# Depthwise convolution of a transformer kernel: all eight channel tiles' filter sums on TensorE, between the tiles of the product ahead of it

## The reference, cut to what matters

```python
def conformer_conv(h, w_pw1, b_pw1, w_dw, b_dw, ln_g, ln_b, w_pw2, b_pw2):
    u = h @ w_pw1 + b_pw1                    # (256, 1024) @ (1024, 2048)
    a, gate = jnp.split(u, 2, axis=-1)
    u = a * jax.nn.sigmoid(gate)             # 1024 channels
    u = causal_depthwise_conv(u, w_dw) + b_dw    # width 31, each channel by itself
    u = jax.nn.silu(layernorm(u, ln_g, ln_b))    # mean and variance over the channels
    return u @ w_pw2 + b_pw2
```

## Time and profile before

| | us or share |
|---|---|
| the profiled execution's own time | 1320.58 |
| its span in the trace | 1319.2 |
| TensorE busy | 1213.2 (92%) |
| VectorE busy | 959.4 (73%) |
| ScalarE busy | 653.0 (49%) |
| mean granted TensorE clock | 0.972 |
| last matmul of pw1 starts at | 69.45 |
| TensorE's convolution begins, mean's last matmul done | 69.66, about 103.6 |
| last matmul of pw2 starts at | 137.21 |

### The profile page before, as it was taken

One profiled execution on the slowest core, in us unless ns is written; L12 is line 12 of the kernel. 1 busy time (PEld: TensorE's weight loads), 2 busy tenths in 40 slices (PEclk: granted clock), 3 DMA queues, 4 the chain that ended last, 5 costly groups with the idle time before them and its releaser, 6 DMA issues.

```text
span 1319.2 us, 24769 instructions
## 1 busy us (share of the span) xinstructions
PE 1213.2 (92%) x9796; PEld 1152.0 (87%) x9796; DVE 959.4 (73%) x1853; ACT 653.0 (49%) x1142; POOL 109.0 (8%) x106
## 2 busy tenths in 40 slices
PE   5988899999998999999977878999988778999999
PEld 4957899999987999999866778999988667999999
DVE  5966598869776888779896558888875554766743
ACT  5316554445446544445556545445445664544531
POOL 2000100002000200004001112000011122100000
PEclk9989899999999999999998989999989988999999
DMA  7587687877853687777633326777855322555551
GB/s 275 158 192 104 209 306 255 260 261 267 265 168 130 217 263 254 248 264 259 212 107 103 96 80 205 260 265 243 301 183 176 117 88 81 181 187 179 189 191 65
DMA packets 81127, 259.36 MB, mean 197 GB/s; under 512 B 8905, under 2 KB 20425, under 8 KB 81013
## 3 DMA queue, kind: packets, MB, share of 16 engines
q1 hardware_dynamic: 81012, 257.79, 61.5%
HBM read 252.68 MB, written 5.08 MB: 195 GB/s over the span
## 4 chain that ended last, share of the span: by engine, by line
PE 70%; DVE 18%; ACT 5%; issue 3%; DMA 1%; POOL 0%; DVEq 0%; ACTq 0%
PE ps L521 63%; DVE wlo L1188 6%; DVE CV L1194 1%; PE ps L582 1%; DVE X L1194 1%; DVE aacc L1194 1%; ACT HH L840 1%; DMA raw<-wall 1%; PE ps L617 1%; ACT tmp L840 1%; ACT oS L840 1%; DVE tmp L1532 1%; PE ps L621 1%; DVE HL L1188 1%; PE ps L689 1%
## 5 line engine op out<-in xcount | busy, mean ns | idle before, releaser
L521 PE MATMUL ps<-HH,whi 128*128 128x256 f32 (+1 forms) x2152 | 626.6, 291 | 32.5 <-DVE wlo L1188 12.5
L521 PE MATMUL ps<-HH,wlo 128*128 128x256 f32 (+1 forms) x2152 | 616.1, 286 | 0.0
L521 PE MATMUL ps<-HL,whi 128*128 128x256 f32 (+1 forms) x2152 | 615.8, 286 | 0.0
L840 ACT ACTIVATE whi<-raw 128x1024 fp32r<-128x1024 f32 x363 | 381.0, 1057 | 335.9 <-PE ps L521 332.1
L1188 DVE TENSOR_TENSOR wlo<-raw,whi 128x1024 fp32r<-128x1024 f32 x363 | 444.2, 1229 | 38.0 <-ACT whi L840 37.6
L521 PEld LDWEIGHTS ps<-HH,whi 128*128 128x128 f32 x2152 | 417.0, 194 | 51.3 <-issue 19.6
L521 PEld LDWEIGHTS ps<-HL,whi 128*128 128x128 f32 x2152 | 416.9, 194 | 0.6
L521 PEld LDWEIGHTS ps<-HH,wlo 128*128 128x128 f32 x2152 | 416.3, 193 | 0.0
L521 PE MATMUL ps<-GH,whi 128*128 128x256 f32 x704 | 198.5, 282 | 0.6 <-DVE bcol L1414 0.5
L521 PE MATMUL ps<-GL,whi 128*128 128x256 f32 x704 | 197.8, 281 | 0.0
L521 PE MATMUL ps<-GH,wlo 128*128 128x256 f32 x704 | 197.8, 281 | 0.0
(11 more groups left out here) (207 smaller groups left out, 976.7 us busy)
## 6 DMA issues: line engine op xcount, KB each, us to landing
raw<-wall SPq DMA_DIRECT2D x363, 512.0 KB, 4.2
araw<-ada SPq DMA_DIRECT2D x96, 512.0 KB, 4.7
UR<-uscr SPq DMA_DIRECT2D x24, 142.0 KB, 3.2
scratch<-bvec SPq DMA_DIRECT2D x1, 3072.0 KB
oBB<-kbias SPq DMA_DIRECT2D x16, 192.0 KB, 2.5
aTB<-scratch SPq DMA_DIRECT2D x12, 128.0 KB, 2.5
X<-x_in SPq DMA_DIRECT2D x2, 512.0 KB, 5.8
out<-X SPq DMA_DIRECT2D x8, 128.0 KB, 2.9
```

What stands on the lines that cost most here:

```text
L521: ins = pe.e.matmul(o, l, r, start=(kt == p.order[0] and i == 0), stop=(kt == p.order[-1] and i == 2))
L840: ac.then_inc(ac.e.activation(o, i, func, **kw), sem)
```

## The change

- All eight channel tiles are convolved by TensorE. VectorE's 62 tap instructions are gone.
- Channel tile j is convolved behind pw1 tile 2j + 5 (`TAPS_AFTER = 4`), so tiles 0 to 5 lie between the tiles of pw1 or right behind its last, 6 and 7 behind that. Directly behind channel tile j stands one matmul of the channel sum, for tile j - 1. Only the sum of tile 7 stands at the end.
- DG becomes a ring of three (it waits for the convolution three before), and VectorE writes U ahead of DG. ScalarE's CV copies move in between its pw1 steps.
- SyncE: U is written out at nt = 2j + 2 and read back at nt = 2j + 3, for all eight; no reads are left for behind the loop. The 3 MB write still stands behind the last of them.

```diff
-CONV_DVE = (0, 1)
-CONV_PE = tuple(j for j in range(KD) if j not in CONV_DVE)
+TAPS_AFTER = 4
@@ TensorE
+                def taps(j):
+                    bk = bank[5 + j % 2]
+                    pe.wait_ge(S.dg, j + 1)
+                    pe.wait_ge(S.ur[j % 3], 64 * (j // 3 + 1))
+                    if j >= 2:
+                        pe.wait_ge(S.cva, j - 1)
+                    for m in range(8):
+                        for r in range(4):
+                            ins = pe.e.matmul(bk[32 * r:32 * r + 32, 0:T], DG[j % 3][:, 8 * r + m, :],
+                                              UR[j % 3][:, r, 4 * m:4 * m + T], start=(m == 0), stop=(m == 7))
+                    pe.then_inc(ins, S.cvt)
+                    if j:
+                        channel_sum(j - 1)
+                def channel_sum(j):
+                    pe.wait_ge(S.bv, 1)
+                    pe.wait_ge(S.cva, j + 1)
+                    return pe.e.matmul(bank[7][:, 0:T], ones[:, :], CV[:, j, :], start=(j == 0), stop=(j == KD - 1))
                 def after(nt):
+                    j, odd_tile = divmod(nt - TAPS_AFTER, 2)
+                    if odd_tile and j >= 0:
+                        taps(j)
...
-                for n, j in enumerate(CONV_PE):
...
+                for j in range((16 - TAPS_AFTER) // 2, KD):
+                    taps(j)
+                pe.then_inc(channel_sum(KD - 1), S.lnt)
@@ VectorE
-                    if nt >= 4:
-                        for _ in range(4):
-                            tap()
...
                         stt(U[:, n, 30:30 + T], t[:, :], V("bp1", n), TMP[(nt - 1) % 8][:, :], ALU.add, ALU.mult, S.u)
+                        dv.wait_ge(S.wq, 16)
+                        dv.wait_ge(S.id32, 3)
+                        if n >= 3:
+                            dv.wait_ge(S.cvt, n - 2)
+                        tt(DG[n % 3][:, :, :], id32[:, :].unsqueeze(1).broadcast_to([P, 32, 32]),
+                           wq[:, n, :].unsqueeze(2).broadcast_to([P, 32, 32]), ALU.mult, S.dg)
-                while taps:
-                    tap()
@@ SyncE
             def taps_out(n):
-                sp.wait_ge(S.u, CONV_PE[n] + 1)
+                sp.wait_ge(S.u, n + 1)
...
-            for nt in range(17):
+            for nt in range(18):
                 if nt < 16:
                     lows(low_to("pw1", nt))
...
-            for n in range(3, len(CONV_PE)):
-                taps_in(n)
+                if nt % 2 == 0 and nt:
+                    taps_out(nt // 2 - 1)
+                if nt % 2 and nt > 1:
+                    taps_in(nt // 2 - 1)
             sp.wait_ge(S.bv, 1)
             load(scratch, bvec[:, :].unsqueeze(1).broadcast_to([12, P, 512]), S.bd)
```

More of the change, by code:

```diff
@@ L333, in __init__ @@
         self.ara = [new(f"ara{i}") for i in range(ARAW)]
-        self.uw = [new(f"uw{i}") for i in range(len(CONV_PE))]
+        self.uw = [new(f"uw{i}") for i in range(3)]
         self.ur = [new(f"ur{i}") for i in range(3)]
@@ L352, in __init__ @@
         self.eps, self.id32, self.uz, self.dg, self.sig, self.u = new("eps"), new("id32"), new("uz"), new("dg"), new("sig"), new("u")
-        self.relm, self.bv, self.cvt, self.cva, self.cvd = new("relm"), new("bv"), new("cvt"), new("cva"), new("cvd")
+        self.relm, self.bv, self.cvt, self.cva = new("relm"), new("bv"), new("cvt"), new("cva")
         self.lnt, self.lnx, self.lnq, self.lnf, self.lns, self.lnh, self.lnl = (
@@ L410, in program @@
             CV = sb("CV", [P, KD, T], F32, st)
-            DG = {j: sb(f"DG{j}", [P, 32, 32], F32, st) for j in CONV_PE}
+            DG = [sb(f"DG{i}", [P, 32, 32], F32, st) for i in range(3)]
             UR = [sb(f"UR{i}", [P, 4, UW], F32, st) for i in range(3)]
@@ L925, in convolution, with taps @@
             def convolution():
+                def taps(j):
+                    ac.wait_ge(S.cvt, j + 1)
+                    act(CV[:, j, :], bank[5 + j % 2][:, 0:T], ACT.Identity, S.cva, bias=V("bdw", j))
                 for kt in range(KD):
@@ L938, in convolution @@
                         act(TMP[nt % 8][:, :], TMP[nt % 8][:, :], ACT.Sigmoid, S.sig, bias=V("bp1", 8 + nt // 2))
-                for n, j in enumerate(CONV_PE):
-                    ac.wait_ge(S.cvt, n + 1)
-                    act(CV[:, j, :], bank[5 + n % 2][:, 0:T], ACT.Identity, S.cva, bias=V("bdw", j))
+                    j, odd_tile = divmod(nt - TAPS_AFTER, 2)
+                    if odd_tile and j >= 0:
+                        taps(j)
+                for j in range((16 - TAPS_AFTER) // 2, KD):
+                    taps(j)
                 warm()
@@ L1307, in convolution @@
             def convolution():
[L1308 to L1318, removed]
                 dv.then_inc(dv.e.memset(epsb[:, :], EPS), S.eps)
@@ L1352, in convolution @@
                     if nt % 2:
[L1353 to L1358, removed]
                         dv.wait_ge(S.sig, n + 1)
@@ L1841, in taps_out @@
             def taps_out(n):
-                sp.wait_ge(S.u, CONV_PE[n] + 1)
+                sp.wait_ge(S.u, n + 1)
                 sp.wait_ge(S.uz, 2)
-                load(uscr[n], U[:, CONV_PE[n], :], S.uw[n])
+                load(uscr[n], U[:, n, :], S.uw[n % 3])
             def taps_in(n):
@@ L1848, in taps_in @@
                     sp.wait_ge(S.cvt, n - 2)
-                sp.wait_ge(S.uw[n], 16)
+                sp.wait_ge(S.uw[n % 3], 16 * (n // 3 + 1))
                 for c in range(4):
@@ L2042 @@
     scratch = nc.dram_tensor("scratch", (12, P, 512), F32, kind="Internal").ap()
-    uscr = nc.dram_tensor("uscr", (len(CONV_PE), P, 31 + T), F32, kind="Internal").ap()
+    uscr = nc.dram_tensor("uscr", (KD, P, 31 + T), F32, kind="Internal").ap()
     out = nc.dram_tensor("out", (P, KD, T), F32, kind="ExternalOutput").ap()
```

## The result

The changed kernel is slower: median 1330.0 us (1328.23 to 1331.15) against 1321.62, ratio 1.0068 with a 95% interval of 1.0047 to 1.0089. Timed again beside the experiments it was 1.0062 (1.0044 to 1.0080). The forecast was 1330.2.

What follows compares the result with a forecast made beforehand. Bound: the 3 MB write's end, which sets weight unit 25's landing and so gu0's start. Write shifted 9.1 us: 1320.58 + 9.1 = 1329.7, or 1330.8 from the median; forecast 1330.2, likeliest 1327 to 1335, wider 1322 to 1336.

Steps and rivals of the forecast that it cites:

- The bound: Path to gu0: the 3 MB write's end sets when weight unit 25 lands; landing moves 9.1 us, from 133.2 to 142.3.
- T: Moment from which TensorE's gu0 matmuls run without a gap; forecast to move as a whole with unit 25, 9.1 us.
- The size of the shift: 3 MB write before gu0: 9.1 us later by its data's start, 10.9 by its issue; 9.1 taken, bounds 6.5 to 14.
- Pw1: TensorE's pw1 with channel tiles, sums, passages and a 1.0 us stall added: ends at 90.8, bounds 89.0 and 95.
- The last U: Behind pw1: last channel tile's write-out issued at 91.9, read-back at 96.5, 3 MB write at 98.2.
- channel tile 7 can start at 98.9, its data lands at 100.9: 2 idle: TensorE behind pw1: 2 us wait ahead of the last channel tile; mean done at 105.4, 1.8 later than 103.6.
- 2.79 us idle didn't lower it, 3.56 did: Clock rival, pw1 stops lowering TensorE to 1.2 GHz: evidence from earlier idle times; one half-clock stretch costs about 2.8 us.
- Nothing of that shows: Pw2 begins 2.4 us later, its last matmul starting at 139.6, but this stays hidden before unit 25's landing at 142.3.
- The balance on TensorE alone is about nothing: TensorE: 2 added tiles cost 6.9 us, stalls and clock give back 9.2, two new stalls take 3.
- The reason for the wait: Before gu0: unit 25 sits behind the 3 MB write in the same queue, landing 2.3 us after its end.
- rival 2: TensorE dearer: tile-width switches cost 0.8 us not 0.1, or reads late; write shifts 15, time 1336; chance 0.11.
- Rival 1: Write doesn't hold unit 25, whose 13.02 us count from its own issue; time 1323.0 or 1319.5; chance 0.14.

Runs made afterwards that it cites:

- e1: Kernel before, convolution untouched, the write repeating the bias table 158 times and not 128; ratio 1.0075, 1329.3 us.
- e7: Changed kernel with channel tiles 0 and 1 back on VectorE, 2 to 7 on TensorE inside pw1, e5's order on SyncE, full write; ratio 1.0002.
- e10: The changed kernel itself, unaltered, timed and profiled again beside the experiments; ratio 1.0062 to the kernel before.
- e3: Changed kernel with a small write of 23 copies and not 128; ratio 1.0016 to the kernel before.
- e2: Kernel before with a small write of 23 copies and not 128, bias reads laid out to fit; ratio 0.9978.
- e5: Changed kernel, full write, U's write-out and read-back ahead of the step's weight load in SyncE's pw1 loop; ratio 1.0053.
- e6: Changed kernel with e5's order on SyncE and the small write of 23 copies; ratio 0.9981.
- e9: Changed kernel with the full 3 MB write issued from ScalarE's DMA queue behind its pw1 loop, not SyncE's; ratio 1.0222.
- e4: Changed kernel with the full 128-copy write issued from ScalarE's DMA queue at its step 5 of pw1; ratio 1.0248.

## Why the prediction was right

- **The bound.** The write's end and unit 25's landing were to move by 9.1 us, T as a whole with them: 9.9 measured at T, 9.0 in the span. e1 (the write alone) and e7 (an earlier mean, the write where it was) show it from both sides. That 1330.2 lies 0.2 us from the measured 1330.0 is in part luck: T moved by more than forecast, and about as much was lost again behind it.
- **The size of the shift.** I took the 9.1 us by which the write's data start later, not the 10.9 of its issue. Measured, the issue moved by 11.2 and the landing by 9.9: the landing came 45.8 us after the write's issue before and 44.6 in the changed kernel. So four reads ahead of it, and not twelve, gave back 1.3 us of the 1.8 that I had counted.
- **Pw1.** Forecast end 90.8, measured 89.95. Channel tile 0 waited 1.17 us for its read-back (I took 1.0); that is luck, for pw1 tile 5 ended at 39.4 and not 40.9, and the write-out took 1.9 us to the next issue and not 3.7 to 5.7. A round took 9.96 us against 5.74 + 3.45 + 0.46 + 0.2 = 9.85: a channel tile and a lone sum cost 3.59 and 0.63, passages included.
- **The last U.** Write-out issued at 91.86 (91.9), read-back at 96.77 (96.5), the 3 MB write at 98.55 (98.2); unit 25 at 143.10 (142.3). The first hit has two errors in it that cancel: pw1 ended 0.85 us sooner, and SyncE, busy until 91.81 with issuing the reads of channel tile 6, came 0.7 us late to a U that was ready at 91.16.
- **Incomplete, and too small:** "channel tile 7 can start at 98.9, its data lands at 100.9: 2 idle". In the first profile the idle 2.2 us came ahead of channel tile 6, whose read-back stood behind weight unit 24, and after it the clock fell, 1.7 us more for that tile. So the mean moved by 3.8 us and not 1.8. In e10 both tiles waited, 1.20 and 1.69 us, without that fall, and the mean moved by 2.6. Nor is the forecast's pair "2.79 us idle didn't lower it, 3.56 did" a limit: here 2.23 us stood ahead of the fall. I had given the later read-backs "over 6 us" in hand; that of channel tile 6 had none, since between its issue at 89.29 and its use only channel tile 5 and a sum were left to do.
- **"Nothing of that shows"** was right in the changed kernel and needs a bound: with the small write e3 stands 5.0 us above e2. The change as it stands costs TensorE's side some 5 us and the write's side 9 to 10; T takes the later one. "The balance on TensorE alone is about nothing" was too low for the changed kernel (the mean 2.6 to 3.8 us later) and by the times comes true only with e5's order (e6 against e2).
- **The reason for the wait.** I put it down to the place in one queue. The landing behind the write is shown; but the queue alone isn't its cause, for on another queue (e9) transfers were held up as well. What is, stays open.
- **The other rivals.** Dearer passages (rival 2) are out by the round. Its sum has a slip: seven switches at 0.7 us are 4.9 and not 6, so its time was 1335. Rival 1's way (landing from its own issue) is out by e1.

## What to carry to other kernels

Before you shorten a stage, look for the large transfer that is issued at its end: its end may set the next stage, and moving work inside the stage moves its issue. Ask then how large the transfer needs to be; here a fifth of it was enough, and only with it did an earlier mean count. When work goes from an engine that is 11 us behind to the one that is the bound, count the stalls that it fills against the work added and the new stalls that it makes: here 9.2 us against 6.9 of work, 1.2 of a stall in pw1 and 2.9 to 3.9 of new stalls and clock behind it, a loss. The order of the transfers on the engine that issues them decided that last part: with the other order e5 has none of it.

## What the runs showed of the hardware

- A write of 3.15 MB from 12 partitions in pieces of 2 KB runs at 76 to 81 GB/s; weights right behind it come at 365 to 406.
- While it runs, a DMA on another queue takes up to 5.0 us to issue (e9) and up to 22.3 us to land (e4; 20.4 in e9), whether it moves 142 or 512 KB. On the write's own queue a weight unit takes up to 5.0 us to issue too.
- With the same instructions, the idle time behind pw1 was 2.79 and 3.56 us in the profile of the kernel before and 4.3 and 1.7 to 2.0 us in those of e1 and e2. The half-clock stretch then lay in one channel tile ahead of a wait and not in three behind it, and the mean was done 2.5 to 2.7 us earlier.
